# Products without use at the heads of the stages, branch gates in the tile of the forget gates, and attention steps half a tile apart

## The reference

```python
def hybrid_layer(x, norm_g, w_in, b_forget, ...):
    xn = rms_norm(x, norm_g)
    z = xn @ w_in
    (qa, ka, va, fa, ga, xb, gb, qc, kcc, vcc, ksc, vsc, kwc, vwc, gate_c, gc,
     ud, vd, gd, mg) = jnp.split(z, split_at, axis=-1)
    y_a = fox_attention(rms_norm(heads(qa), qn_a), rms_norm(heads(ka), kn_a), heads(va), fa + b_forget)
    y_b = rg_lru(xb, conv_w, conv_b, ...)
    y_c = nsa_attention(rms_norm(heads(qc), qn_c), kcc, vcc, ksc, vsc, kwc, vwc,
                        jax.nn.sigmoid(gate_c).reshape(B, S, 3, NSA_HEADS), ...)
    y_d = spatial_gating(ud, vd, ...)
    ys = jnp.stack([y_a * silu(ga), y_b * silu(gb), y_c * silu(gc), y_d * silu(gd)], axis=2)
    proj = jnp.einsum('bsnw,nwd->bsnd', ys, w_branch)
    merged = jnp.sum(jax.nn.sigmoid(mg.reshape(B, S, N_BRANCHES, D)) * proj, axis=2)
    return x + merged @ w_out
```

## Time and profile before

| | |
|---|---|
| median of 3 runs | 1910.02 us (1908.94 to 1912.17) |
| the profiled execution | 1916.41 us, of that span 1914.7 |
| PE busy | 1732.7 us, 90% of the span |
| DVE busy | 1348.5 us, 70% |
| ACT busy | 857.1 us, 45% |
| granted clock of PE, mean | 0.953 |
| weights read | 235 MB, 123 GB/s |

### The profile page before, as it was taken

One profiled execution on the slowest core, in us unless ns is written; L12 is line 12 of the kernel. 1 busy time (PEld: TensorE's weight loads), 2 busy tenths in 40 slices (PEclk: granted clock), 3 DMA queues, 4 the chain that ended last, 5 costly groups with the idle time before them and its releaser, 6 DMA issues. The chain is left out here.

```text
span 1914.7 us, 26205 instructions
## 1 busy us (share of the span) xinstructions
PE 1732.7 (90%) x10080; PEld 1470.3 (77%) x10080; DVE 1348.5 (70%) x2528; ACT 857.1 (45%) x1502; POOL 49.9 (3%) x113
## 2 busy tenths in 40 slices
PE   4799997768999998988899898999998998999997
PEld 2688875556788876867688776888897897888997
DVE  6677773547799999867995477489964554655585
ACT  2523335534444542226454465333344466564541
POOL 1800000000000000000000000000000000000000
PEclk9899998879999998999999899999998989999998
DMA  8343340013223226642454101355454444334442
GB/s 311 108 146 116 124 136 22 1 44 121 77 92 107 89 89 197 209 159 96 163 198 143 55 1 54 124 165 154 153 187 148 148 150 132 111 122 130 146 150 93
DMA packets 65493, 237.96 MB, mean 124 GB/s; under 512 B 7327, under 2 KB 8792, under 8 KB 65112
## 3 DMA queue, kind: packets, MB, share of 16 engines
q1 hardware_dynamic: 64600, 234.70, 37.7%
q10 hardware_dynamic: 768, 1.58, 0.2%
HBM read 234.94 MB, written 1.05 MB: 123 GB/s over the span
## 5 line engine op out<-in xcount | busy, mean ns | idle before, releaser
L445 PE MATMUL banks<-m,weights_high 128*128 128x256 f32 (+1 forms) x4336 | 1056.3, 337 | 78.1 <-DVE weights_low L477 27.9
L445 PEld LDWEIGHTS banks<-m,weights_high 128*128 128x128 f32 x4336 | 744.3, 193 | 175.8 <-issue 32.2
L445 PE MATMUL banks<-m,weights_low 128*128 128x256 f32 (+1 forms) x2168 | 721.1, 333 | 0.0
L477 DVE TENSOR_TENSOR weights_low<-weight_ring,weights_high 128x1024 fp32r<-128x1024 f32 x294 | 357.6, 1223 | 268.8 <-ACT weights_high L472 267.9
L445 PEld LDWEIGHTS banks<-m,weights_low 128*128 128x128 f32 x2168 | 418.7, 193 | 39.7
L472 ACT ACTIVATE weights_high<-weight_ring 128x1024 fp32r<-128x1024 f32 x294 | 310.4, 1057 | 270.5 <-PE banks L445 238.5
L594 DVE SCALAR_TENSOR_TENSOR m<-m,columns 128x189 f32<-128x189 f32 (+4 forms) x856 | 321.6, 453 | 21.8 <-ACT m L546 21.7
L737 DVE SCALAR_TENSOR_TENSOR m<-weight_ring,m 128x1024 bf16<-128x1024 f32 x184 | 225.1, 1224 | 18.0 <-DMA weight_ring<-in_weights 12.5
L545 ACT ACTIVATE m<-banks,columns 128x512 f32<-128x512 f32 (+1 forms) x120 | 83.2, 694 | 308.5 <-PE banks L445 308.3
L445 PE MATMUL banks<-m,weight_ring 128*128 128x256 f32 x704 | 153.9, 382 | 2.4 <-ACT m L862 2.4
L445 PEld LDWEIGHTS banks<-m,weight_ring 128*128 128x128 f32 x704 | 134.9, 192 | 21.4 <-ACT m L862 2.8
(11 more groups left out here) (362 smaller groups left out, 1611.6 us busy)
## 6 DMA issues: line engine op xcount, KB each, us to landing
weight_ring<-in_weights SPq DMA_DIRECT2D x434, 512.0 KB, 3.6
x<-in_tokens SPq DMA_DIRECT2D x1, 2048.0 KB, 14.6
m<-in_cmp_w SPq DMA_DIRECT2D x1, 2048.0 KB, 7.4
m<-in_cond SPq DMA_DIRECT2D x2, 512.0 KB, 4.6
out<-x SPq DMA_DIRECT2D x1, 1024.0 KB, 4.8
columns<-in_columns SPq DMA_DIRECT2D x1, 633.0 KB
m<-in_rg_w ACTq DMA_DIRECT2D x1, 512.0 KB, 7.5
m<-in_spatial_w ACTq DMA_DIRECT2D x1, 512.0 KB
```

The source lines that it names most:

```text
L445: mm = pe.matmul(out, lhsT, rhs, start=p.start and i == 0, stop=p.stop and i == len(passes) - 1)
L477: dve.tensor_tensor(w_lo[:, g % PARTS, :], K.ring[:, PLACE[PRODUCT_BLOCKS[g]] % RING, :], w_hi[:, g % PARTS, :].bitcast(F32), ALU.subtract ...
```

## The change

- `run_products` takes `fill=(a, b)`. PE issues `a` products of the identity with a triangle of ones, 128x128x128 in f32, into bank 0 when a block opens, and `b` more ahead of the first product of a down stage, ahead of its wait. Nothing reads them. The numbers: even_in 24, even_out 8, ffn0 14 and 22, ssd_in 16, ssd_out 8, ffn1 11, in2 8, out2 22; branch2 none.
- The 24 gate columns move into the tile of fa, at rows 32 to 55. The two gate items and their 8 weight tiles go. A step of ACT copies rows 32 to 55 out, `TURN_GATE` transposes them in two pieces on PE (bank 3), and `GATE` takes the sigmoid of both on ACT. Later items stand two earlier.
- `SCORES` stands at item 22 instead of 23 and waits for the first of four scaled sets and the last root, where it waited for the last scaled set. The steps behind it move with it; by items they are now SHIFT 23, EXP 24, WEIGH 26, TURN 27, KEEP 27, where va is 23 and 24, vs 25 and 26, vd 27 and 28. FORGET and FORGET_SUM keep their numbers 23 and 25.
- Of the attention steps, the second turn of a pair is one tick later and behind the next score; weigh, the first turn, the copy of the second turn on ACT and the store on DVE are one tick later too.

```diff
--- before.py
+++ after.py
@@ -326,14 +326,14 @@
     return groups
 
 
-def run_products(K, rounds, mods=None, prepare=None, beside=None, banks=BANKS, acc_slots=8):
+def run_products(K, rounds, mods=None, prepare=None, beside=None, banks=BANKS, acc_slots=8, fill=(0, 0)):
 
 
 
 
 
     with K.scope():
-        _run_products(K, rounds, mods, prepare, beside or Beside(), banks, acc_slots)
+        _run_products(K, rounds, mods, prepare, beside or Beside(), banks, acc_slots, fill)
 
 
 def first_together(rounds, n=TOGETHER):
@@ -410,7 +410,13 @@
     with nc.Block() as block:
         @block.tensor
         def _(pe):
+            def idle(n, bank):
+
+                for _ in range(n):
+                    pe.matmul(K.bank[:, bank, 0:P], K.ident[:], K.tri_f[:], start=True, stop=True)
+
             e, seen, posts_seen = 0, -1, False
+            idle(fill[0], 0)
             for r in rounds:
                 for j in range(len(r)):
                     if e + j >= banks:
@@ -422,6 +428,8 @@
                         if prepare and j == 0 and e * len(it.products) + k < prepare.n:
                             pe.wait_ge(*prepare.ready.at(e * len(it.products) + k + 1))
                         if it.of_posts and not posts_seen:
+                            if j == 0 and k == 0:
+                                idle(fill[1], e % banks)
                             pe.wait_ge(*posted.at(k + 1))
                         b = p.tile // TPB - first
                         plain = first + b in PLAIN
@@ -1148,7 +1156,7 @@
                 r[0].of_posts = True
             run_products(K, first_together(rounds) + down, mods,
                          Normalise(K, t0, f"ffn_g{layer}", (layer, 24, 32), plain=h),
-                         SumSquares(K, t0, first=len(rounds)), BANKS - 1)
+                         SumSquares(K, t0, first=len(rounds)), BANKS - 1, fill=(11, 0) if layer else (14, 22))
 
 
 
@@ -1162,7 +1170,8 @@
                           for name, base in (("gg", 0), ("mq", 4)) for j in range(4)])
         run_products(K, first_together(residual_items(K, "even_out", KD, lambda k: K.h_parts(T, k), 0,
                                                       lambda m, which: K.mod[:, 0, 16 + m, which:which + 1])),
-                     (modulator, blocks_of("mod0")[MOD_EVEN:]), prepare=parts, beside=SumSquares(K, 0), banks=BANKS - 1)
+                     (modulator, blocks_of("mod0")[MOD_EVEN:]), prepare=parts, beside=SumSquares(K, 0), banks=BANKS - 1,
+                     fill=(8, 0))
 
 
 def even_features(K):
@@ -1230,7 +1239,7 @@
     tokens(lambda i: put(f["mo"][:, i, :], ACT.Sigmoid, after=gla.outputs_made))
     rows = [f[name][:, j, :] for name in ("mq", "mk") for j in range(4)] + [f["lf"], f["li"]]
     run_products(K, first_together(rounds), (modulator, blocks_of("mod0")[MOD_FIRST:MOD_EVEN]),
-                 Normalise(K, 0, "mix_g0", (0, 0, 8), rows, rstd=f["lf"]), gla, banks=4, acc_slots=4)
+                 Normalise(K, 0, "mix_g0", (0, 0, 8), rows, rstd=f["lf"]), gla, banks=4, acc_slots=4, fill=(24, 0))
 
 
 CHUNK_ORDER = ([0, 1, 2, 3], [1, 0, 3, 2])
@@ -1906,7 +1915,7 @@
             parts = Split(K, [(xl[:, c, :], *K.h_parts(LAT, c)) for c in range(KI)], normed)
             run_products(K, residual_items(K, "ssd_out", KI, lambda k: K.h_parts(LAT, k), CTX,
                                            lambda m, which: K.mod[:, 1, 16 + m, which:which + 1]), prepare=parts,
-                         beside=SumSquares(K, CTX), banks=BANKS - 1)
+                         beside=SumSquares(K, CTX), banks=BANKS - 1, fill=(8, 0))
 
 
 def ssd_projection(K, zs, xl, xc, bt, ct, dcol, rows, state, mods):
@@ -1933,7 +1942,7 @@
                             lambda act, bank, c=c: act.activation(zs[:, c, :], bank[:, 0:LAT], ACT.Silu))])
         tile += KD
     run_products(K, first_together(rounds), mods, prepare=Normalise(K, 0, "mix_g1", (1, 0, 8)), beside=steps, banks=4,
-                 acc_slots=SSD_ACC)
+                 acc_slots=SSD_ACC, fill=(16, 0))
 
 
 SSD_ACC = 6
@@ -2375,13 +2384,15 @@
 
     for name, n, func in IN2:
         if name == "ud":
-            rounds.append([Item(tile_products(tile, KD, h, LAT),
-                                lambda act, bank: act.activation(f["fa"][0:8, :], bank[0:8, 0:LAT], ACT.Identity,
-                                                                 bias=K.col("b_forget", rows=slice(0, 8)), scale=1.0))])
+            def empty(act, bank):
+                act.activation(f["fa"][32:56, :], bank[32:56, 0:LAT], ACT.Copy)
+                return act.activation(f["fa"][0:8, :], bank[0:8, 0:LAT], ACT.Identity,
+                                      bias=K.col("b_forget", rows=slice(0, 8)), scale=1.0)
+
+            rounds.append([Item(tile_products(tile, KD, h, LAT), empty)])
             tile += KD
             item_of["fa"] = item
             item += 1
-            token_round("gate", 24, ACT.Sigmoid)
             token_round("va", BW, ACT.Copy)
             token_round("vs", 256, ACT.Copy)
             token_round("vd", BW, ACT.Gelu)
@@ -2395,7 +2406,7 @@
         item += n
     spare = [f[name][:, j, :] for name in ("ga", "gb", "gc") for j in range(KB)]
     run_products(K, first_together(rounds), prepare=Normalise(K, CTX, "norm2", None, spare),
-                 beside=HybridSteps(K, f, item_of), banks=3)
+                 beside=HybridSteps(K, f, item_of), banks=3, fill=(8, 0))
 
 
 class Scratch:
@@ -2416,11 +2427,11 @@
 class HybridSteps(Beside):
 
 
-    SIDE_BEGIN, SIDE_LOAD = 32, 20
+    SIDE_BEGIN, SIDE_LOAD = 30, 18
 
     def __init__(self, K, f, item_of):
         Beside.__init__(self)
-        self.sparse = SparseSteps(K, f, Scratch(f["mg"][:, 0:24, :]))
+        self.sparse = SparseSteps(K, f, item_of, Scratch(f["mg"][:, 0:24, :]))
         self.attention = AttentionSteps(K, f, item_of, self.sparse)
         self.side = SideBranches(K, f, SideWeights(K), [f[name] for name in ("ga", "gb", "gc", "gd")])
         self.f, self.item_of = f, item_of
@@ -2459,7 +2470,7 @@
                 dve.tensor_tensor(gate, gate, branch[:, j, :], ALU.mult)
 
     def steps(self, name, eng):
-        self.attention.free = self.free
+        self.attention.free = self.sparse.free = self.free
         return {"tensor": self.attention.tensor_steps, "scalar": self.attention.scalar_steps,
                 "vector": self.attention.vector_steps, "gpsimd": self.attention.no_steps}[name](eng)
 
@@ -2473,7 +2484,7 @@
 
 
 
-    BEGIN, SPACING = 62, 7
+    BEGIN, SPACING = 58, 7
     SCORE, TURN, OUT = 4, 6, 7
 
     def __init__(self, K, f, item_of, sparse):
@@ -2566,15 +2577,15 @@
         for p in range(n + 1):
             at = self.BEGIN + self.SPACING * p
             yield at
-            if p:
-                turn(p - 1, 1)
             if p < n:
                 score(p)
             if p:
-                yield at + 3
+                yield at + 1
+                turn(p - 1, 1)
+                yield at + 4
                 weigh(p - 1)
             if p < n:
-                yield at + 5
+                yield at + 6
                 turn(p, 0)
 
     def scalar_steps(self, act):
@@ -2589,7 +2600,7 @@
         for p in range(n + 1):
             at = self.BEGIN + self.SPACING * p
             if p:
-                yield at + 1
+                yield at + 2
                 keep(p - 1, 1)
             if p < n:
                 yield at + 2
@@ -2643,7 +2654,7 @@
                         ins = dve.tensor_scalar(self.prob[:, e, cols], self.prob[:, e, cols], sums[:, t, e:e + 1], None, ALU.mult)
                 ins.then_inc(*self.normed.up())
             if p:
-                yield at + 4
+                yield at + 5
                 store(p - 1)
 
 
@@ -2664,11 +2675,11 @@
     SWAP, OWN, SWAPPED = 2, 3, 6
     HIDDEN, SILU, TURN_HIDDEN, KEEP_HIDDEN = (8, 9), 11, 12, 13
     KEYS, KEY_SQUARE, VALUES, KEY_SUM, KEY_ROOT, KEY_SCALE = 15, 16, 16, 18, 19, 21
-    FORGET, FORGET_SUM = 23, 25
-    SCORES, SHIFT, EXP, WEIGH, TURN, KEEP = 23, 24, 25, 27, 28, 29
-
-    def __init__(self, K, f, scratch):
-        self.K, self.f = K, f
+    FORGET, FORGET_SUM, TURN_GATE, GATE, GATE_BANK = 23, 25, 24, 25, 3
+    SCORES, SHIFT, EXP, WEIGH, TURN, KEEP = 22, 23, 24, 26, 27, 27
+
+    def __init__(self, K, f, item_of, scratch):
+        self.K, self.f, self.item_of = K, f, item_of
         S = self.SLOT
 
         self.sq, self.rt = f["mg"][:, 28:32, :], f["mg"][:, 24:28, :]
@@ -2689,7 +2700,7 @@
          self.logged, self.hidden, self.silued, self.keyed, self.key_squared, self.key_summed, self.key_rooted,
          self.normed) = K.counts(16)
         (self.valued, self.placed, self.scored, self.shifted, self.exped, self.ready, self.turned, self.kept, self.summed_up,
-         self.vector_step, self.scalar_step, self.pool_step, self.hid_turned, self.hid_kept) = K.counts(14)
```

(22 more changed lines are left out.)

4 lines of the change are left out of this document (2 added, 2 removed).

## The result

The changed kernel takes 1883.53 us (median of 4 runs, 1879.87 to 1884.18), the kernel before beside it 1909.48: ratio 0.9861, 95% interval 0.9847 to 0.9875, so 26 us (24 to 29) faster. The forecast was 1880 in a range of 1872 to 1896. The profiled execution took 1882.93 us with a span of 1881.2. Against the profiled execution of before that is 33.5 us less, 7.5 more than the medians; where these come from is the first thing that the experiments had to find.

A forecast was written before the change was run, and what follows sets the result against it. PE was taken as the bound, through its waits and its half-clock stretches. Idle products 5.7, gate tile 14.2 and attention steps 10.4 summed to 30.3 us, so 1910.0 - 30 = 1880 us, range 1872 to 1896.

The forecast's parts named there:

- rival 4: Idle products do not pipeline, 0.55 us or more each at full clock: kernel slower, 1918 us; chance 0.04.
- rival 5: Out2's opening is no barrier for PE, so its 22 idle products run in idle time: 1874 us; chance 0.05.
- Rival 1: At the heads, real products start at half clock despite idle products: heads -9.9 instead of +5.7, 1896 us; chance 0.12.
- The out2 term: At out2, all 22 idle products stand behind the opening, on PE's path: 4.9 us lost.
- The heads: Where stages of products begin at half clock, idle products bring full clock: 5.7 us gained in sum, out2's loss included.
- 1.4 late: At even_out, 8 idle products end 1.4 us after the first real product could begin; gain still 0.9 us.
- The 0 for ssd_out: Ssd_out's head waits for DVE's split of each part at either clock, so idle products gain 0 there.
- 7.3 + 1.8 - 1.3: Gate terms: narrow gate products removed 7.3 us, scores at full clock 1.8, new wait of SCORES for ACT's root -1.3.
- The va term: The va round at full clock gains 3.1 us, less 0.8 for half a chance of one dip.
- Rival 3: Forget steps hold up ACT, PE waits around vd and the clock dips: gates give 10, 1884 us; chance 0.12.
- rival 2: Attention waits move instead of going, as ACT keeps its order: attention gives 3 us, 1887 us; chance 0.15.
- differences carry over: In the sum, the 30.3 us found on the profiled span was taken off the 1910.0 us median.

The follow-up runs named there:

- before again: The kernel before, unchanged, run once more for a second profile: 1912.05 us against 1911.77, ratio 1.0005; its profiled execution took 1908.48 us.
- no idle: The changed kernel with no idle products at all, gate tile and attention order kept: 1883.85 us, 0.9861 of the kernel before.
- experiments 6 and 7: Changed kernel with 28 out2 idle products at the end of branch2's list, 1877.76 us; with 17 there and one weight block cut ahead of the opening, 1873.83 us.
- idle products only: The kernel before with the idle products of the change and nothing else: 1907.87 us, 0.9986 of the kernel before.
- experiment 11: The changed kernel with the step TURN back at item 26 instead of 27, ahead of the vd round: 1889.63 us, 0.9893 of the kernel before.
- experiment 8: The changed kernel with the old order and ticks of the attention steps: 1896.67 us, 0.9927 of the kernel before.
- the halves: Changed kernel with only the second turn and its copy moved, 1891.28 us; with only weigh, first turn and store moved, 1895.54 us.

## Why the prediction held, and where its terms were off

**What was right.** The bound (PE's waits and its clock) and the mechanisms all showed as named: full clock in the first 5 us of ffn0 and ssd_in, out2's first product 6.59 us behind its opening, va straight behind the scores, TURN's wait gone, attention waits under 3 us. The price of an idle product, 0.224 us, was measured as 0.22 to 0.23, so rival 4 (0.5 and more) and rival 5 are out. Rival 1 is out for ffn0 and ssd_in.

**Idle products: 5.7 forecast, 0 to 3 measured.** The out2 term was right (-4.9; 4.9 to 5.1 by the traces). The heads were oversized. The step that failed is taking the length of each dip from one profile: "half clock from 465.52 to 470.61 goes, gain 2.4". That dip lasted for 5.1 us of products in that execution and for 3.5 in the next. Two profiles without the products (before again, no idle) give for ffn0 1.6 (2.4 forecast), ssd_in 2.0 (2.9) and ffn1 1.1 (1.4). Even_in's 28 instructions gain 2.5 to 2.8, but its first product comes 1.0 us later in the changed kernel (0 to 1.1 in the others with idle products), so 1.5 to 1.8 net for 1.5 forecast. Even_out's 36 gain 1.0 to 1.2, and its first product comes 1.5 us later (2.0 in six of nine others with idle products): a loss of 0.2 to 1.0 for a gain of 0.9 forecast. The "1.4 late" there was too little by the forecast's own price: 8 products at half clock are 3.4 us, 2.0 more than the gap. The 0 for ssd_out was right, though it was read from a row that begins 3.3 us behind the head's first product. In2's head gains 2.5 over these two (1.5 forecast), but 12 us behind it a dip appears that kernels without idle products don't have and all that have them do, at 1.2 us. I had said nothing of it. The 22 ahead of ffn0's down products were forecast at 0 under the wait for weights_low; they cost 0.2 to 0.4. Together these stretches give some 2 us. Of the rest, 1.5 us was lost in the rest of ssd_in in the profile of the changed kernel, but not in each one with idle products (197.0 in experiments 6 and 7): that is chance, as is what the mixer's stretch shows beyond the later start of even_out.

**The gate tile: 14.2 forecast, 12.3 from the first profile of before.** Against "before again" it is 9.1, against "idle products only" 10.5. The ratio of the changed kernel is worth 26.6 us; less the attention's 12.6 and the idle products' 0 to 3 it leaves 11 to 14. Term by term, from the first profile of before and, in brackets, the second: from fa to va 7.7 (7.3) was gained, for 7.3 + 1.8 - 1.3 = 7.8 forecast, and the new wait for the root was 1.21 us against 1.3. The va term was off: 3.1 less 0.8 for a dip forecast, 1.0 (-0.3) measured, since one dip stayed behind the scores (granted clock 0.87 over the round). For vs and vd, 4.9 for TURN's wait, dip and transposes less 0.3 and 0.5 for what is new was forecast, 4.1; 3.7 (2.1) measured. That TURN's old place would have come to cost 6.1 (experiment 11) I had not seen. Rival 3 was not seen: ACT does the forget steps at the end of va, but PE waited nowhere at vd for low parts by over 0.3 us.

**The attention: 10.4 forecast, 14.1 in every trace, 12.6 by the ratios.** The move removed nearly all: 9.9 of 11.0 us of waits and the whole dip. I had kept 0.9 + 1.3 us of waits, counted the dip of 3.2 by half, and charged part of each tick to ACT's keep. ACT did not follow as late as feared; rival 2 (gain 3) is refuted by experiment 8. What I had not seen is that the halves do more together (14.1) than one by one (6.6 + 3.4). It looks as if each kind of wait had hidden part of the other, since with one gone the other is longer; for the first half that fits, while in the second the turns also stand closer together, so the reason is argued and not shown.

**The sum.** 30.3 was forecast as a difference of profiles. Those differ by 33.5, the medians by 26. The step "differences carry over", from a profile 6.4 us above its median to the median, failed: most of those 6.4 us were stretches that ran badly once, and I had booked parts of them (heads, va, vd) as gains of the change. That the forecast came within 3.5 us of the time is in part luck: idle products too high by 3 to 6 and the gate tile by 0 to 3, the attention too low by 2 to 4.

## What to carry to other kernels

Work without use paid here only where the engine would have waited anyway; behind an opening that the engine itself waits for, each product costs its full 0.22 us, and the place for it is the end of the list before, where it paid 6.3 us here. Price a clock dip from two profiles of the same program, not one, and expect that part of it comes back later. Of two chained handovers move both: each alone gained 6.6 and 3.4 us, together 14.1. And when an engine is made faster, look at its next wait: with the scores at full clock PE waited 5.0 us at TURN's old place (experiment 11) instead of 2.8.
